# Where scale and shift of a norm are applied: ScalarE or VectorE, and two weight splits among its pairs

## The reference

```
c_act = jax.nn.silu(c)
for l in range(DEPTH_2):
    mod = c_act @ w_mod[l] + b_mod[l]
    shift, scale, gate = jnp.split(mod, 3, axis=-1)
    h = rmsnorm(x, norm_gain[l]) * (1.0 + scale[:, None, :]) + shift[:, None, :]
    proj = h @ w_in[l]
    ...
    x = x + gate[:, None, :] * y
```

## Time and profile before

| | |
|---|---|
| median of 3 runs | 2072.11 us (2061.25 to 2075.68) |
| the profiled execution | 2069.3 us |
| its span, first to last instruction | 2067.5 us |
| mean granted TensorE clock | 0.949 |
| PE / DVE / ACT busy | 93% / 83% / 60% |
| norm 2, first product to end of the last hlo | 1263.06 to 1280.35 us |
| norm 3, the same | 1675.44 to 1692.74 us |

### The profile page before, as it was taken

How to read it: one execution, slowest core, us unless ns; L and a number is a source line. 1 busy time by engine, 2 the same in 40 slices (tenths; PEclk the granted TensorE clock), 3 DMA queues, 4 the chain that set the end, 5 groups by cost and what they waited for, 6 DMA issues and landing times. The chain is left out here.

```text
span 2067.5 us, 34027 instructions
## 1 busy us (share of the span) xinstructions
PE 1919.1 (93%) x13292; PEld 1784.4 (86%) x13292; DVE 1713.3 (83%) x2198; ACT 1246.5 (60%) x1927; POOL 280.2 (14%) x182
## 2 busy tenths in 40 slices
PE   5999989999999988999999997999989879999898
PEld 5789889999998888899989976998888769988887
DVE  6886978877998898888998887789879876898776
ACT  5566644744666656555666667456766574566573
POOL 0000031041110012311000100222101002222010
PEclk9998999999999989999999998899999889999999
DMA  7686666767999776788889876768779867686785
GB/s 240 206 286 204 214 226 212 258 217 265 311 354 355 232 264 211 259 294 299 295 303 337 291 277 209 242 201 290 242 245 326 302 196 247 204 277 223 268 300 204
DMA packets 270764, 536.88 MB, mean 260 GB/s; under 512 B 31880, under 2 KB 40973, under 8 KB 269581
## 3 DMA queue, kind: packets, MB, share of 16 engines
q1 hardware_dynamic: 270317, 532.62, 77.0%
q10 hardware_dynamic: 288, 2.10, 0.3%
HBM read 532.55 MB, written 2.10 MB: 259 GB/s over the span
## 5 line engine op out<-in xcount | busy, mean ns | idle before, releaser
L150 PE MATMUL ps<-hh_r,w 128*128 128x256 f32 x3384 | 860.9, 294 | 47.2 <-DVE ring_r L1832 27.4
L150 PEld LDWEIGHTS ps<-hh_r,w 128*128 128x128 f32 x3384 | 669.4, 198 | 61.0 <-DVE ring_r L1832 35.0
L150 PE MATMUL ps<-hlo,ring_r 128*128 128x256 f32 x2856 | 715.8, 289 | 0.0
L1832 DVE SCALAR_TENSOR_TENSOR ring_r<-ring,w 128x1024 fp32r<-128x1024 f32 (+1 forms) x455 | 568.2, 1263 | 158.2 <-ACT w L1381 156.3
L1381 ACT ACTIVATE w<-ring 128x1024 fp32r<-128x1024 f32 (+1 forms) x455 | 470.9, 1051 | 215.1 <-PE ps L150 85.7
L150 PEld LDWEIGHTS ps<-hlo,ring_r 128*128 128x128 f32 x2856 | 567.0, 199 | 1.1 <-issue 0.7
L150 PE MATMUL ps<-hlo,AR_r 128*128 128x256 f32 x1064 | 260.3, 284 | 0.0
L1832 DVE SCALAR_TENSOR_TENSOR AR_r<-AR,w 128x1024 fp32r<-128x1024 f32 x167 | 211.0, 1275 | 46.2 <-ACT w L1381 45.2
L150 PE MATMUL ps<-w,AR_r 128*128 128x512 f32 x584 | 236.1, 404 | 7.1 <-DVE AR_r L1832 7.1
L1381 ACT ACTIVATE w<-AR 128x1024 fp32r<-128x1024 f32 x167 | 173.8, 1055 | 67.3 <-PE ps L150 25.4
L150 PEld LDWEIGHTS ps<-hlo,AR_r 128*128 128x128 f32 x1064 | 206.8, 194 | 0.6 <-issue 0.5
(11 more groups left out here) (212 smaller groups left out, 2724.0 us busy)
## 6 DMA issues: line engine op xcount, KB each, us to landing
ring<-in_w_in SPq DMA_DIRECT2D x294, 512.0 KB, 4.9
ring<-in_w_mod SPq DMA_DIRECT2D x124, 512.0 KB, 5.5
ring<-in_w_up SPq DMA_DIRECT2D x113, 512.0 KB, 5.5
AR<-in_w_in SPq DMA_DIRECT2D x75, 512.0 KB, 5.2
ring<-in_w_out SPq DMA_DIRECT2D x65, 512.0 KB, 5.9
AR<-in_w_up SPq DMA_DIRECT2D x63, 512.0 KB, 5.7
ring<-in_w_down SPq DMA_DIRECT2D x62, 512.0 KB, 5.7
AR<-in_w_mod SPq DMA_DIRECT2D x56, 512.0 KB, 5.6
```

The lines of the kernel that those rows point to most:

```text
L150: return e.matmul(o, l, x, start=start, stop=stop, skip_group_check=True)
L1832: return e.scalar_tensor_tensor(o, a, s, b, op0, op1)
```

## The change

In norms 2 and 3, VectorE now applies gain, scale and shift. After the product with 1/rms (a new event "over") it issues two `tensor_scalar` with two operations each, one for each channel tile, in place in the staging buffer; ScalarE then makes hhi of the pair with one `first`, as in the norms of the first block. In VectorE's order the two new instructions stand behind the `second` of the pair before. gsp and shp go away with the two small instructions that made them. In the planner, all norms without a list of splits (norms 1, 2 and 3) split one chunk behind segment 5 and one behind segment 7, if a chunk and a buffer are there.

```diff
@@ norm() of the planner
             if 2 * seg - 2 in meanwhile:
                 ensure(meanwhile[2 * seg - 2])
+            if not meanwhile and seg in (5, 7) and next_split() is not None:
+                ensure(next_split())
@@ norm of scalar_program
                 e.wait_ge(*norm_dve.after("s", n, k))
-                if n < 2:
-                    first(flat2(hhi[:, k:k + 2, :]), s_).then_inc(*norm_act.step("hi", n, k))
-                else:
-                    for kk in range(2):
-                        c = k + kk
-                        fn(hhi[:, c, :], s_[:, 256 * kk:256 * kk + 256], ACT.Identity, bias=shp[:, c:c + 1], scale=gsp[:, c:c + 1])
-                        q = fn(s_[:, 256 * kk:256 * kk + 256], s_[:, 256 * kk:256 * kk + 256], ACT.Identity,
-                               bias=modcm[:, n - 2, c:c + 1], scale=gsc[:, c:c + 1])
-                    q.then_inc(*norm_act.step("hi", n, k))
+                first(flat2(hhi[:, k:k + 2, :]), s_).then_inc(*norm_act.step("hi", n, k))
@@ rstd of vector_program
-                stt(gsc, modcm[:, L, 16:32], 1.0, cols("ng", 16 * L, 16), ADD, MUL).then_inc(*rstd_dve.step("gain0", n))
-                e.wait_ge(*rstd_dve.after("gain0", n))
-                ts(gsp, gsc, 1.0 / (SPL + 1.0), MUL)
-                ts(shp, modcm[:, L, 0:16], 1.0 / (SPL + 1.0), MUL).then_inc(*rstd_dve.step("gain", n))
+                stt(gsc, modcm[:, L, 16:32], 1.0, cols("ng", 16 * L, 16), ADD, MUL).then_inc(*rstd_dve.step("gain", n))
+                e.wait_ge(*rstd_dve.after("gain", n))
@@ norm of vector_program
                         q = stt(s_[:, 256 * kk:256 * kk + 256], hh[:, k + kk, :], col(("ln1", "ln2")[n], k + kk), bc, MUL, MUL)
+                    q.then_inc(*norm_dve.step("s", n, k))
                 else:
-                    q = tt(pair(s_), hh[:, k:k + 2, :], mid(bc, 2), MUL)
-                q.then_inc(*norm_dve.step("s", n, k))
+                    tt(pair(s_), hh[:, k:k + 2, :], mid(bc, 2), MUL).then_inc(*norm_dve.step("over", n, k))
             if seg > 1:
                 k = 2 * seg - 4
                 e.wait_ge(*norm_act.after("hi", n, k))
                 second(flat2(hlo[:, k:k + 2, :]), st(J, f"s{k}"), flat2(hhi[:, k:k + 2, :])).then_inc(*norm_dve.step("lo", n, k))
+            if 1 <= seg <= 8 and n >= 2:
+                k = 2 * seg - 2
+                e.wait_ge(*norm_dve.after("over", n, k))
+                for c in (k, k + 1):
+                    o = st(J, f"s{k}")[:, 256 * (c - k):256 * (c - k) + 256]
+                    q = ts(o, o, gsc[:, c:c + 1], MUL, modcm[:, n - 2, c:c + 1], ADD)
+                q.then_inc(*norm_dve.step("s", n, k))
```

More of the change, by code:

```diff
@@ L280, in program @@
     ret_sm = [sm[:, 412 + 12 * i:424 + 12 * i] for i in range(4)]
-    gsp, shp = sm[:, 464:480], sm[:, 480:496]
     GQ, GK, GV = carve(0, 8, S), carve(2048, 8, S), carve(4096, 8, S)
```

## The result

| | before | changed |
|---|---|---|
| median of 5 runs each, us | 2072.87 (2061.25 to 2075.68) | 2089.3 (2086.1 to 2090.74) |
| ratio, 95% interval | 1 | 1.0099 [1.0078, 1.012] |
| the profiled execution / its span, us | 2069.3 / 2067.5 | 2087.73 / 2085.9 |
| mean granted TensorE clock | 0.949 | 0.943 |
| norm 2: first product, end of last hlo | 1263.06, 1280.35 (17.3) | 1264.37, 1286.83 (22.5) |

The changed kernel is slower by about 1% (20 us by the ratio; the two medians are 16.4 us apart). Counted from the first product of each norm to the end of its wi, layer 1 takes 53.40 us instead of 45.07 (+8.3) and layer 2 takes 52.55 instead of 43.98 (+8.6). These 16.9 us are nearly all of the 18.4 us by which the profiled span grew.

The account below looks back on a forecast made before the run. TensorE, busy 93%, was taken as the bound, with the norm's end setting wi's start through the gate's load. Norm 2 (3.4 + 2.8) and norm 3 (4.3 + 3.6) add 14.1 us to 2072.1, giving 2086; range 2064 to 2098.

Parts of the forecast that it names:

- What bounds the kernel, and the gate: Behind norms 2 and 3: the norm's end, through the gate's load and later loads, sets wi's start; gate to landing 14.2 us.
- Rival A: Behind norms 2 and 3: landing catches up with the later gate, long waits vanish; up to 18.4 us faster, 2054; chance 0.12.
- The work of a pair: Pair loop of norms 2 and 3: 1.92 us instead of 1.97, last hlo 1.1 us earlier without any split.
- A split among the pairs: In norms 2 and 3: each split costs the norm 2.69 us, 1.64 of it idle VectorE; last hlo 4.3 us later.
- What TensorE gains on its first chunks: Behind norm 2: the 6.5 us wait becomes three smaller ones, 1.5 us won by the sixth chunk; about 2 in norm 3.
- The start of wi: Behind norms 2 and 3: wi starts later because its landing follows the later gate, +3.4 and +4.3 us.
- wi at half clock: After standing, all 64 matmuls of wi run at half clock, 13.76 us: +2.8 and +3.6 us.
- Rival B: wi is shifted later but starts at full clock after the shorter stands: 7.7 us slower, 2080; chance 0.18.
- Norm 1: Two splits make VectorE end this batch some 2.2 us later, but TensorE's ready chunks cover it: 0 us.
- Rival D: Norm 1 and the blocks behind pay too as TensorE's lead runs out: 2 to 10 us more, up to 2100; chance 0.10.
- The sum: Later starts and half clock of wi behind norms 2 and 3: 3.4 + 2.8 and 4.3 + 3.6, together 14.1 us.
- Rival C: Later stretches where TensorE waits for VectorE absorb the loss, nothing lasting: 2070 to 2076; chance 0.13.

Follow-up runs that it names:

- gate_late_after: Changed kernel with the gate's load moved from behind the norm to ahead of the second qi block, behind wi; ratio 1.0015 to the kernel before.
- arith_only: Changed kernel without the splits among the pairs of norms 1 to 3, VectorE still applying scale and shift; ratio 1.0002 to the kernel before.
- apart2: Changed kernel with each split's halves apart: ScalarE's behind segments 4 and 6, VectorE's behind 5 and 7; ratio 1.0045 to the kernel before.
- apart_all_gate_late: Changed kernel, splits with halves apart behind segments 3 to 6 of norms 2 and 3, none in norm 1, gate's load behind wi; 2056.18 us, ratio 0.9939.
- fill40: Changed kernel with 40 useless matmuls of 256 columns on TensorE ahead of each ki block; ratio 1.0065 to the kernel before.

## Why the prediction was right

The forecast was 2086 us, 0.7% slower; measured were 2089.3 and a ratio of 1.0099 [1.0078, 1.012]. The mechanism held in layers 1 and 2, and three terms were too small: the new instructions, the start of wi in layer 1 and, as far as can be told, norm 1, which was put at 0.

**What bounds the kernel, and the gate.** Right. gate_late_after shows it: the norm as long as in the changed kernel, and the loss nearly gone (with the gate's 1 MB moved as well). Rival A (the landing catches up with the gate) fell: gate to landing is 15.07 and 14.16 us, not below 10.

**The work of a pair.** The mis-sized term is tensor_scalar: 0.408 us, where I took 0.35 from the form with one operand; the bounds 0.35 to 0.48 held it. The loop is 2.04 us instead of 1.92, which is 7 x 0.12 = 0.84 us a norm. arith_only shows that this decides nothing.

**A split among the pairs.** Right: 2.68 us measured, 2.69 forecast, with 1.64 us of idle VectorE in both. apart2 and apart_all_gate_late show that the idle time comes from the two halves standing together. The norm grew by 5.2 us, which is the forecast 4.3 and the 0.84 of the loop.

**What TensorE gains on its first chunks.** Three smaller waits came (1.73, 4.11 and 0.94 us in norm 2). Together they are 6.8 us, so less than the forecast 1.5 us was won by the sixth chunk: it starts 24.0 us behind the first product (at 1288.37) and started some 24.6 behind it before (near 1287.7, by the earlier trace rows). TensorE came to wi 1.2 and 0.6 us later behind the first product than before (35.32 instead of 34.14 us, and 33.29 instead of 32.66), where I had let it come when it did. Neither enters the sum, since the copies came later still.

**The start of wi.** Forecast +3.4 and +4.3 us, measured from the first product +5.6 (39.75 instead of 34.14) and +5.1 (38.90 instead of 33.80). In layer 2 the difference is the 0.84 of the loop. In layer 1 it is 2.2: again 0.84, and a landing that came 1.3 us later behind the gate (15.07 instead of 13.81 us). By the stretches, 15.07 us at 306 GB/s are 4.6 MB, and before it was 13.81 us at 284 GB/s, or 3.9 MB: more data passed in between. SyncE's queue shows the send of the chunk that landed there, in the kernel before first and in the changed kernel behind the dots:

```profile
1289.86 0.37 SPq L964 DMA_DIRECT2D ring<-in_w_in  x1
...
1293.02 0.74 SPq L965 DMA_DIRECT2D ring<-in_w_in  x1
```

Behind the gate it went out 6.2 us later instead of 9.5, but it took 8.9 us to land instead of 4.3. The sends now follow each other faster, and later ones pass beside it: 3.8 MB had been sent up to and with it in both kernels (estimated from the sizes of the sends), against the 4.6 and 3.9 MB that were moved when it landed.

**wi at half clock.** Right: 13.65 us in both layers against 13.76 forecast, +2.7 and +3.5 against +2.8 and +3.6. Rival B (clock kept, 2080) fell, and in layer 1 fill40 shows the clock as a cost of its own. In layer 2 that wasn't shown, since the filler did not bring the clock back.

**Norm 1.** Put at 0, and this is the term that was missing. Its two splits made the norm longer by 4.5 us (11.4 to 15.9 us from first product to last hlo, 2 x 2.27 as forecast), and its own chunks came in time, but TensorE waits 1.77 us at 730.75. I had looked at the eight chunks of the first block only, and left it at a remark that VectorE, busy 98% of that stretch, may stay behind; the wait at 730.75 fits that remark. Rival D had named this. It holds in part at most, with 2.7 us by the means over the traces, beside the forecast and not in its place, and its size is not settled.

**The sum.** 16.9 us in the two layers instead of 14.1: 2.1 more in layer 1, 0.7 more in layer 2. The span's 18.4 has 1.5 more, which single traces can't place: norm 1 begins at 677.83 before and 680.74 after, with nothing changed ahead of it, and from 672.5 to 681.6 over all traces of this study. From norm 1 to norm 2 the trace of before is among the longest of its kind (585.2 us), and that of after among the shortest (583.6). By the ratio, the changed kernel is 20 us slower (16 to 25 by the interval), which leaves about 3 for norm 1 and all else, within the noise. The slowdown was forecast as 14.1 us and measured as 16.4 by the two medians and 20 by the ratio, so that the forecast of 2086 lies only 3 us off is in part luck: in the later batches the kernel before had medians of 2067.6 to 2070.0, where I had counted from 2072.1. Rival C (absorbed later) fell: between the end of wi in layer 1 and the first product of norm 3 only 0.5 us came back.

## What to carry to other kernels

Before moving work into a gap, look at what is queued behind the end of the stretch that gets longer: here the gate's DMA waited in order for the norm, every later load waited behind it, and two norms that were 5.2 us longer each cost 17 us; with the same DMA moved to a later place they were nearly free. A step that two in-order engines do one after the other costs the second one its wait as well (2.68 us for a split against 0.94 with other work between the halves). A wait of TensorE can be paid twice, once standing and once at half clock behind it.

## What the runs showed of the hardware that I had not expected

- A tensor_scalar of 128x256 in float32 with two per-partition operands takes 0.408 us, with one operand 0.346.
- The 64 matmuls of wi with 16 columns take 13.65 us at a granted clock of 0.50, 8.85 us at a mean of 0.79 (fill40) and 10.93 us at 0.63 (before). Where they started at full clock, the clock still fell while they ran without a gap: in the kernel before it was 1.00 from 1297.20 to 1300.03 us and 0.50 from there to the end of wi at 1308.13.
- In layer 2 of fill40 TensorE had worked at 1.00 without a gap from 1708.00 to 1718.70 us, the wait was only 2.64 us, and the clock was 0.51 all the same. Whether the wait or the work ahead of it decides was not told apart.
